# Convolution weights fetched into another buffer ahead of time, and attention run by pairs of key-value heads, in a decoder layer on eight cores

## The chip, the cores and the metric

The kernel runs on all 8 cores of one Trainium2 chip. Every core runs the same program on its own rows: 2048 prompt rows and 64 rows of new tokens, with all weights read by each core. The metric is the time on the device, in microseconds (us), of the slowest core. TensorE (PE) does the matmuls, ScalarE (ACT), VectorE (DVE) and GpSimd (POOL) the elementwise work. PE, ACT, DVE and POOL each take their instructions in program order; transfers are issued from the queues of SyncE (SP) and POOL.

## The reference

One layer. The input projection gives queries, keys, values, a gated linear unit `u` and two gates. Two branches use them: banded attention with a sink, and a causal depthwise convolution of width 31 with layer norm.

```python
def _sink_attention(q, k, v, mask, sink):
    s = jnp.einsum('nqkgd,nskd->nkgqs', q, k,
                   preferred_element_type=jnp.float32) * ATTN_SCALE
    s = jnp.where(mask, s, NEG)
    sk = sink.astype(jnp.float32).reshape(1, N_KV_HEADS, GROUP, 1, 1)
    m = jnp.maximum(jnp.max(s, axis=-1, keepdims=True), sk)
    e = jnp.exp(s - m)
    den = jnp.sum(e, axis=-1, keepdims=True) + jnp.exp(sk - m)   # sink column absorbs mass
    p = (e / den).astype(v.dtype)
    o = jnp.einsum('nkgqs,nskd->nqkgd', p, v)
    return o.reshape(o.shape[0], o.shape[1], ATT_W)
...
def _conv_tail(ubuf, conv_w, conv_b, cln_g, cln_b, w_conv_o):
    c = lax.conv_general_dilated(ubuf, conv_w[:, None, :], (1,), 'VALID',
                                 dimension_numbers=('NWC', 'WIO', 'NWC'),
                                 feature_group_count=D_CONV) + conv_b
    c = jax.nn.silu(_layernorm(c, cln_g, cln_b))
    return c @ w_conv_o
```

There are 16 query heads of 64 channels on 4 key-value heads, a window of 128, 1024 convolution channels and 2048 model channels. Then `mix = (gate0 * (attention @ w_attn_o) + gate1 * conv) @ w_out`, a residual, and a squared-ReLU MLP of 8192 channels.

## The kernel before

**Groups.** The rows of a core are worked in three groups: group 0 has 5 blocks of 128 rows and the 128 rows ahead of them, group 1 has 6 blocks, group 2 has 5 blocks and the 64 new-token rows (`G.SA`). A group goes through the whole layer before the next begins. All weights come as slabs of 2048 x 512 (`load_slab`, `prefetch`), through three buffers, from the POOL queue.

**Dense steps and side work.** A stage of dense work is a generator that stops after each output tile of 128 channels by half the group's columns: 16 matmuls into one PSUM bank, here called a dense step. `run(main, side, per)` (line 278) lets a second generator take `per` of its steps for each dense step. While attention runs, the main stages are `q_stage(G, 1)`, `ub_stage(G, 0)`, `ua_stage(G, 1)` and `ub_stage(G, 1)`, 8 dense steps each, in banks 0 to 3; banks 4 and 5 take scores, 6 transposes, 7 value products. A dense step of `q_stage` is read out by DVE, one of `ua_stage` by ACT, one of `ub_stage` by ACT (tanh into `ring`) and then by DVE, which waits for `ring`.

**Attention** (`att_stage`). A unit is one block `i` of 128 queries and one key-value head (`kv = 2a + hh`), with its 4 query heads. Head `hh` of a pair `a` lives on channels 0 to 63 or 64 to 127 of the partitions. `S`: 8 score matmuls (4 query heads by two key blocks, 64 rows of the array, 128 columns) into banks 4 and 5; ACT copies one bank to `Sp`, DVE writes the masked other one over it (`copy_predicated`), DVE takes the minimum, and ACT computes 4 exponentials with their sums. `N`: DVE reciprocal, POOL multiply. `Tr`: 4 transposes into bank 6, and DVE spreads them by the mask into `PT`. `V`: 2 value matmuls of 512 columns into one half of the output columns of bank 7; after the second head of a pair ACT or DVE reads the bank out. The loop at the end of `att_stage` runs, in step `k`, `S(k)`, `N(k-1)`, `Tr(k-3)`, `V(k-4)`. In group 2 there are 8 further units (`SUnit`) for the cached keys of the new tokens.

**Convolution** (`conv_stage`). `ub_stage` writes `u` to a scratch in HBM, 4 chunks of 128 channels at a time, once for each half (`us0`, `us1`). `load_x(ch)` reads a chunk back four times, shifted by one row each, into `X`; 4 such buffers are in use. A chunk is then 64 matmuls that use 32 of the 128 array columns each, in turns on the four quarters. The weights of a chunk are 32 x 32 blocks in HBM (`wdb`): chunks 0 and 1 are loaded into `wd0` and `wd1` before attention, chunks 2 to 5 into `wdm`, which lies in `AT`, and chunks 6 and 7 into `wd0` and `wd1` once chunks 0 and 1 are done. `AT` is the buffer that holds attention's `P` and `PT`, so the transfer of `wdm` is issued on SP after the last value product. The eight chunks run beside `gate_stage(G, 0, 0)`, one behind each of its dense steps.

## Time and profile before

| what | us |
|---|---|
| median of 3 runs | 3547.96 |
| lowest and highest | 3545.12, 3552.78 |
| the profiled execution | 3547.48 |
| its span on the slowest core (core 7) | 3545.8 |
| spans of the other cores | 3528.3 to 3543.3 |
| PE busy | 3406.3 (96%) |
| LDWEIGHTS busy | 2202.0 (62%) |
| DVE, ACT, POOL busy | 1052.7, 825.6, 478.2 |

PE is busy for 96% of the span, and most of the rest lies in three places, once in each group: the stretch in which attention runs beside the projections, and the stretch of the convolution behind it. A busy PE is not PE at its peak: the ends of matmuls are modelled, so the distance between the starts of two entries tells more than their durations. The granted clock column (PEclk) is a share of 2.4 GHz, 0.5 being 1.2 GHz.

### The profile page before, as it was taken

The page shows a single profiled execution, that of the slowest core. Times are in us where ns is not written, and L with a number is a line of the kernel's source. Part 1 is how long each engine was busy: PE and PEld are TensorE (multiplying, and loading weights), DVE is VectorE, ACT ScalarE, POOL GpSimd, SP SyncE. Part 2 cuts the span into 40 slices and gives each one's busy share as a digit, 9 for nine tenths or more (in the row PEclk, how much of TensorE's full clock was granted, in tenths as well). Part 3 has the DMA queues.
Part 4 walks back from the last instruction along what each step waited for, and adds up shares of the span by engine and source line. Part 5 has one row for each costly group of instructions (what it writes and reads, how often), then busy time and mean ns, then how long its engine had stood idle before and what let it go on. Part 6 is the DMA issues. An engine that isn't in the chain of part 4 may idle for free.

```text
span 3545.8 us, 62090 instructions; the slowest of 8 cores (3528.3 to 3545.8 us)
## 1 busy us (share of the span) xinstructions
PE 3406.3 (96%) x24208; PEld 2202.0 (62%) x24208; DVE 1052.7 (30%) x1963; ACT 825.6 (23%) x1877; POOL 478.2 (13%) x604
## 2 busy tenths in 40 slices
PE   7979999999999989999999999998889999999997
PEld 5546777777776545666666666664556666666664
DVE  2423222222234434132222222345341222222223
ACT  2443132111101444113210111113431132110103
POOL 0112020011012113003001110121130030000003
PEclk9989999999999999999999999999989999999998
DMA  8775786677778375567666666687776575565553
GB/s 173 121 145 104 138 164 125 127 144 149 141 160 188 79 144 104 111 111 146 115 114 129 131 123 112 135 163 126 139 143 130 113 157 120 121 128 105 110 118 91
DMA packets 83262, 460.61 MB, mean 130 GB/s; under 512 B 7552, under 2 KB 39936, under 8 KB 61568
## 3 DMA queue, kind: packets, MB, share of 16 engines
q0 software_dynamic: 27520, 351.48, 55.8%
q1 hardware_dynamic: 55456, 105.17, 10.7%
q8 instruction: 197, 3.23, 0.4%
q14 instruction: 89, 0.73, 0.1%
HBM read 784.43 MB, written 31.49 MB: 230 GB/s over the span
## 4 chain that ended last, share of the span: by engine, by line
PE 87%; DMA 4%; DVE 3%; ACT 3%; issue 2%; POOL 1%; SPq 0%; ACTq 0%; DVEq 0%; POOLq 0%
PE ps L130 87%; DMA AT<-wdb 2%; ACT AT L130 1%; DVE R L130 1%; DMA yT<-R 1%; DVE TMP L130 1%; DMA MIX<-xm 1%; POOL R L130 1%; ACT TMP L130 1%; ACT R L130 0%; DVE sm L130 0%; SPq L130 0%; DVE AT L130 0%; ACT ring L130 0%; ACT GT L130 0%
## 5 line engine op out<-in xcount | busy, mean ns | idle before, releaser
L130 PE MATMUL ps<-N,w 128*128 128x384 bf16 (+3 forms) x11712 | 1798.3, 315 | 0.0
L130 PEld LDWEIGHTS ps<-N,w 128*128 128x128 bf16 x11712 | 1144.4, 98 | 644.4 <-issue 39.1
L130 PE MATMUL ps<-MIX,w 128*128 128x320 bf16 (+2 forms) x4608 | 688.8, 313 | 0.0
L130 PEld LDWEIGHTS ps<-MIX,w 128*128 128x128 bf16 x4608 | 450.9, 98 | 236.5
L130 PE MATMUL ps<-GT,w 128*128 128x320 bf16 (+2 forms) x3072 | 459.4, 313 | 0.0
L130 DVE SCALAR_TENSOR_TENSOR ring<-ps,TMP 128x320 f32<-128x320 f32 (+2 forms) x384 | 200.7, 524 | 678.6 <-PE ps L130 675.4
L130 DVE TENSOR_TENSOR R<-ps,R 128x320 f32<-128x320 f32 (+2 forms) x384 | 201.4, 524 | 672.0 <-PE ps L130 672.0
L130 PEld LDWEIGHTS ps<-GT,w 128*128 128x128 bf16 x3072 | 300.6, 98 | 157.9 <-issue 0.2
L130 POOL TENSOR_TENSOR TMP<-TMP 128x320 f32<-128x320 f32 (+2 forms) x222 | 209.3, 946 | 434.7 <-ACT TMP L130 434.7
L130 PE MATMUL ps<-R,w 128*128 128x320 bf16 (+2 forms) x1536 | 232.0, 312 | 3.2 <-ACT R L130 3.2
L130 DVE SCALAR_TENSOR_TENSOR GT<-GT,ps 128x320 f32<-128x320 f32 (+2 forms) x192 | 99.5, 520 | 398.6 <-PE ps L130 387.4
L130 ACT ACTIVATE GT<-ps,hbg 128x320 f32<-128x320 f32 (+2 forms) x192 | 105.8, 552 | 435.2 <-PE ps L130 435.2
L130 ACT ACTIVATE GT<-ring 128x320 bf16<-128x320 f32 (+2 forms) x192 | 95.3, 496 | 479.5 <-DVE ring L130 479.5
L130 ACT ACTIVATE TMP<-R 128x320 f32<-128x320 f32 (+2 forms) x240 | 114.9, 488 | 395.1 <-DVE R L130 391.6
L130 ACT ACTIVATE MIX<-ring 128x320 bf16<-128x320 f32 (+2 forms) x192 | 94.7, 496 | 463.5 <-DVE ring L130 463.5
L130 PEld LDWEIGHTS ps<-R,w 128*128 128x128 bf16 x1536 | 150.0, 98 | 83.2 <-issue 4.9
L130 ACT ACTIVATE AT<-TMP,sm 128x129 bf16<-128x129 f32 (+1 forms) x264 | 107.9, 409 | 147.4 <-DVE sm L130 129.6
L130 POOL DMA_DIRECT2D w<-w_dn x48 | 25.9, 539 | 710.4 <-PE ps L130 710.4
L130 POOL DMA_DIRECT2D w<-w_up x48 | 26.3, 547 | 620.9 <-PE ps L130 620.9
L130 POOL TENSOR_TENSOR AT<-AT,sm 128x512 bf16<-128x512 bf16 x64 | 66.4, 1038 | 274.4 <-DVE sm L130 257.8
L130 DVE SCALAR_TENSOR_TENSOR R<-ps,R 128x320 f32<-128x320 f32 (+2 forms) x96 | 50.4, 525 | 176.8 <-PE ps L130 176.8
L130 ACT ACTIVATE N<-R,vec 128x320 bf16<-128x320 f32 (+2 forms) x96 | 56.4, 588 | 195.9 <-DVE R L130 195.9
(104 smaller groups left out, 1409.0 us busy)
## 6 DMA issues: line engine op xcount, KB each, us to landing
w<-w_up POOLq DMA_DIRECT2D x48, 2048.0 KB, 16.9
w<-w_dn POOLq DMA_DIRECT2D x48, 2048.0 KB, 16.3
w<-w_in POOLq DMA_DIRECT2D x45, 2048.0 KB, 15.8
w<-w_ac POOLq DMA_DIRECT2D x12, 2048.0 KB, 17.1
w<-w_out POOLq DMA_DIRECT2D x12, 2048.0 KB, 16.2
AT<-xm SPq DMA_DIRECT2D x32, 384.0 KB, 11.6
AT<-xm SPq DMA_DIRECT2D x32, 352.0 KB, 9.3
MIX<-uscr SPq DMA_DIRECT2D x52, 167.0 KB, 6.3
```

The source lines that it names most:

```text
L130: ins = getattr(engobj, fn[0])(*fn[1], **fn[2])
```

## The change

**Convolution weights.** The chunks 2 to 7 (instead of 2 to 5) go to `wdm`, which now lies in the second part of the gate buffer `GT` and is loaded on SP together with `wd0` and `wd1`, before attention begins. The reloads of `wd0` and `wd1` are gone. To make room, the tail of `u` that is an output goes through `RS`, and the tails of keys and values through `TMP`. The second half of `u` is written to the scratch two chunks at a time, the first two after half of the stage, and `load_x` waits for the write of its own chunk alone.

**Attention by twos.** A `Pair` is both key-value heads of `a` on one block. Its scores come as two steps: `A` does the later key block, 8 matmuls in turns on the row halves, head 0 into bank 4 and head 1 into bank 5, and ACT copies both; `B` does the earlier key block into the same banks, then DVE and ACT follow as before, for both heads. `Tr` does 8 transposes into the two halves of bank 6, and `V` 4 value matmuls in turns on the column halves of bank 7. There are 6 buffers for `P` instead of 4. The loop runs in step `k` first `V(k-3)`, `A(k)`, `N(k-1)`, and after a yield `Tr(k-2)`, `B(k)`. A step of the side work is thus half of a pair, `na` is 4·nb+5 (+8 in group 2) instead of 4·nb+4 (+8), and the `SUnit`s run by twos as well.

```diff
-            ut = gtf[:, 3200:3200 + 768].rearrange("p (k c) -> p k c", c=96)
+            ut = RS[:, 0:768].rearrange("p (k c) -> p k c", c=96)
...
-            hs = slice(hf * 4, hf * 4 + 4)
-            dmas("sp", [(uscr[G.g, hs, :, 0:G.UW].rearrange("k p c -> p k c"), G.uT[:, hs, :])],
-                 reads=[f"uT{c}" for c in range(hf * 4, hf * 4 + 4)], writes=[f"us{hf}"], sem=f"d_us{hf}")
-            if G.SA:
-                dmas("sp", [(sscr[hs].rearrange("k p c -> p k c"), G.ub[:, hs, :, :].rearrange("p k r b -> p k (r b)"))],
-                     reads=["ubs"] + [f"ub{c}" for c in range(hf * 4, hf * 4 + 4)], writes=[f"ss{hf}"], sem=f"d_ss{hf}")
+                if m == 3 or m == 1 and hf:
+                    h0, hs = (ch - 1, slice(ch - 1, ch + 1)) if hf else (0, slice(0, 4))
+                    dmas("sp", [(uscr[G.g, hs, :, 0:G.UW].rearrange("k p c -> p k c"), G.uT[:, hs, :])],
+                         reads=[f"uT{c}" for c in range(h0, ch + 1)], writes=[f"us{c}" for c in range(h0, ch + 1)], sem=f"d_us{ch}")
+                    if G.SA:
+                        dmas("sp", [(sscr[hs].rearrange("k p c -> p k c"), G.ub[:, hs, :, :].rearrange("p k r b -> p k (r b)"))],
+                             reads=["ubs"] + [f"ub{c}" for c in range(h0, ch + 1)], writes=[f"ss{c}" for c in range(h0, ch + 1)],
+                             sem=f"d_ss{ch}")
...
+            place("GATES", [("wdm", 12800, 25088)])
+            wm = gtb[:, 6400:12544].rearrange("p (k a b) -> p k a b", k=6, a=32)
+            dmas("sp", [(wm, wdb[2:8].rearrange("k p a b -> p k a b"))], reads=["wdb"], writes=["wdm"], sem="d_wdm")
             yield
...
-                dmas("sp", pairs, reads=[f"us{ch // 4}"] + ([f"ss{ch // 4}"] if G.SA else []), writes=[f"X{i}"], sem=f"d_X{i}")
+                dmas("sp", pairs, reads=[f"us{ch}"] + ([f"ss{ch}"] if G.SA else []), writes=[f"X{i}"], sem=f"d_X{i}")
...
             yield
-            place("AT", [("wdm", 0, 8192)])
-            wm = AT[:, 0:4096].rearrange("p (k a b) -> p k a b", k=4, a=32)
-            dmas("sp", [(wm, wdb[2:6].rearrange("k p a b -> p k a b"))], reads=["wdb"], writes=["wdm"], sem="d_wdm")
...
-                wk, wv = (f"wd{ch % 2}", wd[ch % 2][:, :, :]) if ch < 2 or ch > 5 else ("wdm", wm[:, ch - 2, :, :])
+                wk, wv = (f"wd{ch}", wd[ch][:, :, :]) if ch < 2 else ("wdm", wm[:, ch - 2, :, :])
...
                 if xl < 8:
                     load_x(xl)
                     xl += 1
-                if ch < 2:
-                    load_wd(ch + 6, wk)
...
-                def S(self):
...
-                    sp = Sp[s2][:, :, 0:128]
-                    do("pool", "tensor_copy", ["cst"], [f"sp{s2}"], out=Sp[s2][:, :, 128], in_=nsk[:, self.kv * 4:self.kv * 4 + 4])
-                    bb = [bank("S"), bank("S")]
-                    for blk in (1, 0):
-                        for g in range(4):
-                            do("pe", "matmul", ["kT", f"q{a}_{i}"], [f"ps{bb[blk]}"], inc=(g == 3), out=ps[bb[blk]][:, g * 128:g * 128 + 128],
+            class Pair:
+                def __init__(self, k, i, a):
+                    self.k, self.i, self.a = k, i, a
+                    self.s3 = [(k % 3) * 2 + j for j in range(2)]
+
+                def scores(self, blk):
+                    i, a = self.i, self.a
+                    for g in range(4):
+                        for j in range(2):
+                            hs = slice(j * 64, j * 64 + 64)
+                            b = rings["S"][j]
+                            do("pe", "matmul", ["kT", f"q{a}_{i}"], [f"ps{b}"], inc=(g == 3), out=ps[b][:, g * 128:g * 128 + 128],
                                lhsT=G.qT[hs, a * 4 + g, i * 128:i * 128 + 128],
                                rhs=G.kT[hs, a, (i + blk) * 128:(i + blk) * 128 + 128], start=True, stop=True)
-                    do("act", "activation", [f"ps{bb[1]}"], [f"sp{s2}"], out=sp, in_=ps[bb[1]][:, :].rearrange("p (g c) -> p g c", g=4),
-                       func=AF.Copy)
-                    do("dve", "copy_predicated", [f"ps{bb[0]}", "msk", f"sp{s2}"], [f"sp{s2}"], out=sp, mask=mpv,
-                       data=ps[bb[0]][:, :].rearrange("p (g c) -> p g c", g=4))
-                    if G.g == 0 and i == 0:
-                        do("dve", "tensor_tensor", ["msk", f"sp{s2}"], [f"sp{s2}"], out=sp, in0=sp, in1=mad, op=ALU.add)
-                    do("dve", "tensor_reduce", [f"sp{s2}"], [f"nm{s3}"], out=sm[:, 0, s3, :], in_=Sp[s2], axis=AX.X, op=ALU.min)
-                    for g in range(4):
-                        do("act", "activation", [f"sp{s2}", f"nm{s3}"], [f"P{s3}_{g}", f"dn{s3}"], out=Pb[s3][:, g, 0:129],
-                           in_=Sp[s2][:, g, :], func=AF.Exp, scale=-1.0, bias=sm[:, 0, s3, g:g + 1],
-                           accum_out=sm[:, 1, s3, g:g + 1])
+
+                def A(self):
+                    self.scores(1)
+                    for j in range(2):
+                        b = rings["S"][j]
+                        do("act", "activation", [f"ps{b}"], [f"sp{j}"], out=Sp[j][:, :, 0:128],
+                           in_=ps[b][:, :].rearrange("p (g c) -> p g c", g=4), func=AF.Copy)
+                    for j in range(2):
+                        kv = 2 * self.a + j
+                        do("pool", "tensor_copy", ["cst"], [f"sk{j}"], out=Sp[j][:, :, 128], in_=nsk[:, kv * 4:kv * 4 + 4])
+
+                def B(self):
+                    self.scores(0)
+                    for j in range(2):
+                        b, s3, sp = rings["S"][j], self.s3[j], Sp[j][:, :, 0:128]
+                        do("dve", "copy_predicated", [f"ps{b}", "msk", f"sp{j}"], [f"sp{j}"], out=sp, mask=mpv,
+                           data=ps[b][:, :].rearrange("p (g c) -> p g c", g=4))
+                        if G.g == 0 and self.i == 0:
+                            do("dve", "tensor_tensor", ["msk", f"sp{j}"], [f"sp{j}"], out=sp, in0=sp, in1=mad, op=ALU.add)
+                        do("dve", "tensor_reduce", [f"sp{j}", f"sk{j}"], [f"nm{s3}"], out=sm[:, 0, s3, :], in_=Sp[j], axis=AX.X, op=ALU.min)
+                        for g in range(4):
+                            do("act", "activation", [f"sp{j}", f"sk{j}", f"nm{s3}"], [f"P{s3}_{g}", f"dn{s3}"], out=Pb[s3][:, g, 0:129],
+                               in_=Sp[j][:, g, :], func=AF.Exp, scale=-1.0, bias=sm[:, 0, s3, g:g + 1],
+                               accum_out=sm[:, 1, s3, g:g + 1])
...
                 def Tr(self):
-                    s2, s3 = self.s2, self.s3
-                    b = bank("T")
-                    for g in range(4):
-                        do("pe", "transpose", [f"P{s3}_{g}", "msk"], [f"ps{b}"], inc=(g == 3), out=psb[b][:, g * 128:g * 128 + 128],
...
+                    b = rings["T"][0]
+                    for j, s3 in enumerate(self.s3):
+                        for g in range(4):
+                            do("pe", "transpose", [f"P{s3}_{g}", "msk"], [f"ps{b}"], inc=(g == 3),
+                               out=psb[b][:, j * 512 + g * 128:j * 512 + g * 128 + 128], in_=Pb[s3][:, g, 0:128], identity=idb[:, :])
+                    for j in range(2):
+                        do("dve", "tensor_tensor", [f"ps{b}", "msk"], [f"PT{j}"],
+                           out=PT[j].rearrange("p (b g q) -> p b g q", b=2, g=4),
+                           in0=psb[b][:, j * 512:j * 512 + 512].rearrange("p (g q) -> p g q", g=4).unsqueeze(1).broadcast_to([128, 2, 4, 128]),
+                           in1=mkq, op=ALU.mult)
...
                     for blk in (1, 0):
-                        do("pe", "matmul", [f"v{i + blk}", f"PT{s2}"], [f"ps{b}"], inc=(blk == 0), out=ps[b][self.hs, :],
-                           lhsT=G.vt[:, i + blk, self.kv * 64:self.kv * 64 + 64], rhs=PT[s2][:, (1 - blk) * 512:(2 - blk) * 512],
-                           start=(blk == 1), stop=(blk == 0))
-                    if self.hh == 1:
-                        evac([f"ps{b}"], [f"q{a}_{i}"], G.qT[:, a * 4:a * 4 + 4, i * 128:i * 128 + 128],
-                             ps[b][:, :].rearrange("p (g q) -> p g q", g=4))
+                        for j in range(2):
+                            kv = 2 * a + j
+                            do("pe", "matmul", [f"v{i + blk}", f"PT{j}"], [f"ps{b}"], inc=(blk == 0 and j == 1), out=ps[b][j * 64:j * 64 + 64, :],
+                               lhsT=G.vt[:, i + blk, kv * 64:kv * 64 + 64], rhs=PT[j][:, (1 - blk) * 512:(2 - blk) * 512],
+                               start=(blk == 1), stop=(blk == 0))
...
             n = len(units)
-            for k in range(n + 4):
-                if G.SA and k in (2, 9):
-                    make_qc(k > 2)
+            for k in range(n + 3):
+                if 0 <= k - 3 < n:
+                    units[k - 3].V()
                 if k < n:
-                    units[k].S()
+                    units[k].A()
                 if 0 <= k - 1 < n:
                     units[k - 1].N()
-                if 0 <= k - 3 < n:
-                    units[k - 3].Tr()
-                if 0 <= k - 4 < n:
-                    units[k - 4].V()
+                yield
+                if G.SA and k in (1, 4):
+                    make_qc(k > 2)
+                if 0 <= k - 2 < n:
+                    units[k - 2].Tr()
+                if k < n:
+                    units[k].B()
                 yield
...
-            na = 4 * G.nb + 4 + (8 if G.SA else 0)
+            na = 4 * G.nb + 5 + (8 if G.SA else 0)
...
```

What stands in a row on TensorE in group 0, beside the first dense steps of `ub_stage(G, 0)`: `ps<-N,w` is a dense step (`x32` are two), `ps<-R` scores, `ps<-idb,AT` transposes, `ps<-AT,R` value products. Before:

```order
L130 MATMUL ps<-N,w 128x336 x32
L130 MATMUL ps<-R 128x128 x8
L130 MATMUL ps<-idb,AT 128x128 x4
L130 MATMUL ps<-AT,R 64x512 x2
L130 MATMUL ps<-N,w 128x336 x16
```

and after:

```order
L130 MATMUL ps<-N,w 128x336 x32
L130 MATMUL ps<-AT,R 64x512 x4
L130 MATMUL ps<-R 128x128 x8
L130 MATMUL ps<-N,w 128x336 x16
L130 MATMUL ps<-idb,AT 128x128 x8
L130 MATMUL ps<-R 128x128 x8
L130 MATMUL ps<-N,w 128x336 x16
```

Where each gap between dense steps held the scores, transposes and value products of one unit each, the gaps now hold in turn value products with scores of a pair, and transposes with scores of a pair; the 8 score matmuls alternate between two banks.

VectorE in the same stage, from one unit to the next (the `ring` rows are readouts of dense steps, `ps4` and `ps5` the scores, `ps6` the transposes). Before:

```order
L130 SCALAR_TENSOR_TENSOR R2<-ring1,GT 128x336
L130 COPY_PREDICATED TMP<-msk,ps4 128x4x128
L130 TENSOR_REDUCE sm<-TMP 128x4
L130 RECIPROCAL sm<-sm 128x4
L130 TENSOR_TENSOR AT<-ps6,msk 128x1024
L130 SCALAR_TENSOR_TENSOR R2<-ring0,GT 128x336
```

and after:

```order
L130 TENSOR_TENSOR AT<-ps6,msk 128x1024 x2
L130 COPY_PREDICATED TMP<-msk,ps4 128x4x128
L130 TENSOR_REDUCE sm<-TMP 128x4
L130 COPY_PREDICATED TMP<-msk,ps5 128x4x128
L130 TENSOR_REDUCE sm<-TMP 128x4
L130 SCALAR_TENSOR_TENSOR R2<-ring0,GT 128x336
L130 RECIPROCAL sm<-sm 128x4 x2
L130 SCALAR_TENSOR_TENSOR R2<-ring1,GT 128x336
```

The reciprocals stood behind the minimum of the next unit and now stand ahead of it; the readout of the transposes stood behind the scores and now stands ahead of them, and a dense readout that waits for ScalarE lies between the minimum of one pair and the scores of the next.

The SP queue in group 0, from the first convolution weights on (`wdb` weights, `uscr` the scratch of `u`). Before:

```order
L130 DMA wd<-wdb 128x1024 x2
L130 DMA uscr<-R 128x4x672
L130 DMA MIX<-uscr 32x4x668 x16
L130 DMA uscr<-R 128x4x672
L130 DMA AT<-wdb 128x4x1024
L130 DMA MIX<-uscr 32x4x668 x4
L130 DMA wd<-wdb 128x1024
```

and after:

```order
L130 DMA wd<-wdb 128x1024 x2
L130 DMA GT<-wdb 128x6x1024
L130 DMA uscr<-R 128x4x672
L130 DMA MIX<-uscr 32x4x668 x16
L130 DMA uscr<-R 128x2x672 x2
L130 DMA MIX<-uscr 32x4x668 x16
```

The block of weights moved from behind the last write of `u` to ahead of the first, the write of the second half became two, and nothing but the loads of chunks stands behind them.


## Rows read from the trace of the kernel before

**Rows 1.** Busy time by stretch: the three attention stretches, columns as its head says.
```profile
core 7: us, PE busy (x) PEld busy (x) DVE busy (x) ACT busy (x) POOL busy (x), PEclk, DMA share, GB/s
106.68:226.54 119.86, 108.49 (x761) 64.93 (x761) 57.14 (x110) 62.03 (x210) 24.96 (x41) 0.91 0.65 113
1170.28:1302.43 132.15, 119.31 (x817) 65.45 (x817) 64.28 (x123) 73.28 (x247) 29.66 (x49) 0.97 0.49 92
2403.30:2552.18 148.88, 122.52 (x961) 70.55 (x961) 77.23 (x195) 71.28 (x243) 25.96 (x42) 0.94 0.66 120
```

**Rows 2.** The same view, the three convolution stretches.
```profile
226.54:277.77 51.23, 38.26 (x641) 25.74 (x640) 6.47 (x14) 18.52 (x39) 11.38 (x13) 0.87 0.70 140
1302.43:1357.40 54.97, 45.36 (x642) 25.77 (x641) 7.32 (x14) 20.83 (x39) 13.46 (x13) 0.91 0.71 143
2552.18:2618.23 66.05, 47.13 (x898) 30.79 (x897) 7.14 (x16) 20.94 (x46) 12.41 (x13) 0.82 0.87 174
```

**Rows 3.** Waits of PE over the whole span: us in total, times, longest.
```profile
PE ps L130 <- DMA AT<-wdb: 34.9, 3, 13.0
```

**Rows 4.** Timeline of PE in convolution: start, us, engine, form, count [idle before].
```profile
228.82 2.36 PE L130 MATMUL ps<-MIX,wd 128*32 128x320 bf16 x64
231.11 2.35 PE L130 MATMUL ps<-N,w 128*128 128x320 bf16 x16
...
250.99 4.02 PE L130 MATMUL ps<-MIX,AT 128*32 128x320 bf16 x64 [12.97 <-DMA AT<-wdb]
...
2590.17 0.24 PE L130 MATMUL ps<-MIX,AT 128*32 128x64 bf16 x4 [4.67 <-issue]
```

**Rows 5.** Timeline of the SP queue at the start of that stretch.
```profile
227.48 0.38 SPq L130 DMA_DIRECT2D uscr<-R  x1
228.02 1.01 SPq L130 DMA_DIRECT2D AT<-wdb  x1
246.47 1.74 SPq L130 DMA_DIRECT2D MIX<-uscr  x4
```

**Rows 6.** Transfers issued in 105:290 us: count, KB each, median us to landing.
```profile
MIX<-uscr SPq DMA_DIRECT2D x32, 167.0 KB, 8.7
...
uscr<-R SPq DMA_DIRECT2D x2, 672.0 KB, 11.3
...
AT<-wdb SPq DMA_DIRECT2D x1, 1024.0 KB, 22.7
```

**Rows 7.** Timeline of PE, one unit of attention between dense steps.
```profile
163.00 0.62 PE L130 MATMUL ps<-R 64*128 64x128 bf16 x8
163.55 0.40 PE L130 MATMUL ps<-idb,AT 128*128 128x128 bf16 x4
163.88 0.62 PE L130 MATMUL ps<-AT,R 128*64 128x512 bf16 x2
164.43 4.73 PE L130 MATMUL ps<-N,w 128*128 128x336 bf16 x32
```

**Rows 8.** Timeline of PE, scores of a new-token unit and what follows.
```profile
2463.39 0.30 PE L130 MATMUL ps<-MIX 64*32 64x256 bf16 x4
...
2463.63 0.40 PE L130 MATMUL ps<-idb,AT 128*128 128x128 bf16 x4
```

**Rows 9.** Timeline of DVE and ACT from one unit's exponentials to the next unit's.
```profile
191.11 0.66 DVE L130 TENSOR_TENSOR AT<-ps,msk 128x1024 bf16<-128x1024 bf16 x1
191.20 0.41 ACT L130 ACTIVATE AT<-TMP,sm 128x129 bf16<-128x129 f32 x1 [1.73 <-DVE sm L130]
...
193.37 0.43 ACT L130 ACTIVATE GT<-ps 128x336 f32<-128x336 f32 x1
...
193.70 0.58 ACT L130 ACTIVATE TMP<-ps 128x512 f32<-128x512 f32 x1
194.38 0.73 DVE L130 COPY_PREDICATED TMP<-msk,ps 128x512 f32<-128x512 int16 x1 [2.01 <-ACT TMP L130]
...
196.01 0.41 ACT L130 ACTIVATE AT<-TMP,sm 128x129 bf16<-128x129 f32 x1 [1.72 <-DVE sm L130]
```

More of the change, by code:

```diff
@@ L232, in build @@
         tf = TMP[:, :]
-        Pb = [AT[:, i * 520:(i + 1) * 520].rearrange("p (g c) -> p g c", g=4) for i in range(4)]
-        PT = [AT[:, 2080 + i * 1024:2080 + (i + 1) * 1024] for i in range(2)]
+        Pb = [AT[:, i * 520:(i + 1) * 520].rearrange("p (g c) -> p g c", g=4) for i in range(6)]
+        PT = [AT[:, 3120 + i * 1024:3120 + (i + 1) * 1024] for i in range(2)]
         atf = AT[:, :].bitcast(F32)
@@ new lines, in N @@
+                def N(self):
+                    for s3 in self.s3:
+                        do("dve", "reciprocal", [f"dn{s3}"], [f"rd{s3}"], out=sm[:, 2, s3, :], in_=sm[:, 1, s3, :])
+                        do("pool", "tensor_tensor", [f"rd{s3}"] + [f"P{s3}_{g}" for g in range(4)], [f"P{s3}_{g}" for g in range(4)],
+                           out=Pb[s3][:, :, 0:128], in0=Pb[s3][:, :, 0:128], in1=sm[:, 2, s3, :].unsqueeze(2).broadcast_to([128, 4, 128]),
+                           op=ALU.mult)
@@ L835, in V @@
                         hs = slice(hh * 64, hh * 64 + 64)
-                        out = ps[b][hs, a * 32:a * 32 + 32]
+                        out = ps[b][hs, o0 + a * 32:o0 + a * 32 + 32]
                         vc = slice(kv * 64, kv * 64 + 64)
```

102 lines of the change are left out of this document (54 added, 48 removed).

## The prediction

> **What bounds the kernel now.** I read the page for the share of PE (96% of the span), then the waits of PE, then the busy time by stretch around them. Two kinds of stretch stand out, once in each group. In the three stretches of attention [rows 1] PE's window is 119.86 + 132.15 + 148.88 = 400.9 us. In the three of the convolution [rows 2] it is 51.23 + 54.97 + 66.05 = 172.3 us. Everything else in the program is dense work that the change doesn't touch. So the sum is made of these 573 us, and the rest of the profiled execution (3547.48 us, of which the span is 3545.8) is carried over. It stands 0.5 us below the median of the runs, so what I subtract from the one I subtract from the other.
>
> **Convolution, what is removed.** PE waits 34.9 us in three waits for `AT<-wdb` [rows 3]. The queue shows why: that transfer is issued at 228.02, behind the last write of `u` and 0.8 us ahead of the first convolution matmul, and takes 22.7 us to land [rows 5, 6]. Moved ahead of attention it has over 100 us. What would the stretch be without it? A chunk of 64 matmuls takes 231.11 - 228.82 = 2.29 us at 320 columns [rows 4], which is also about what a dense step of 16 matmuls takes, since the four column quarters work at once. Eight chunks and eight dense steps are then 16 x 2.29 = 36.6 us in group 0; scaled by the columns (384 in group 1; 352 in group 2, whose chunk has 704 in all) 43.9 and 40.3 us. That leaves 14.6 + 11.1 + 25.8 = 51.5 us of the 172.3 as excess. It is the 34.9 us of waits, the slow clock behind them (the first chunk after the wait takes 4.02 us for 2.36 [rows 4]; the granted clock is 0.87, 0.91 and 0.82 in the three stretches [rows 2]), and, in group 2, waits that the profile lays on nothing, the longest 4.67 us [rows 4].
>
> **Convolution, what is late next.** The loads of chunks 4 to 7. Before, the load of chunk 4 was issued at 246.47, when the write of the whole second half of `u` had landed, 19 us after its issue at 227.48 [rows 5]. With no stall chunk 4 is due four chunk-and-step periods of 4.58 us after 228.82, at 247.1, so the old order would have waited here for the chunk's 8.7 us to landing [rows 6]: without the second edit, the first would return some 8 us per group. With it, chunks 4 and 5 are written four dense steps earlier and their loads wait for a free buffer only, from 231.1 on: 16 us for a transfer of 8.7. Chunk 6 needs the last write, now half as large; if it still takes 19 us it lands at 246.5, and 8.7 us later, at 255.2, the chunk is there, due at 256.3. That is tight, and in group 2 the DMA share is 0.87 [rows 2]. Removing the 22.7 us transfer from the same moments helps. I take 47 of the 51.5 us, and 30 to 52 as the bounds: the low end gives back some 7 us per group for a late chunk. The early transfer, now 1.5 times as large, itself is free: what stands behind it on SP is the first write of `u`, due only at the end of `ub_stage(G, 0)`, and PE's one wait for a transfer in these stretches is the one removed [rows 3]. The moved tails of `u`, keys and values are the same instructions on other buffers that are idle then.
>
> **Attention, PE's work.** One unit is 0.55 us of scores, 0.33 of transposes and 0.55 of value products, from start to start [rows 7]: 1.43 us. A dense step is 4.73 / 2 = 2.37 us at 336 columns, so 2.26, 2.71 and 2.48 at 320, 384 and 352. From the first scores on, the stretches hold 30, 30 and 31 dense steps, 20, 24 and 20 units and, in group 2, 8 new-token units of about 0.9 us (an estimate: 0.24 us for their scores [rows 8], the rest in proportion). PE's work is thus 99 + 116 + 112 = 327 us of 400.9; 74 us are waits and slow clock. What do turns on the row and column halves save? For columns, the convolution shows four quarters at once [rows 4]. For rows the nearest row is the new-token scores: 4 matmuls of 256 columns on two row halves and four column quarters take 0.24 us with 4 small ones from start to start [rows 8], where one alone, at a dense step's 0.148 us for 336 columns, would take 0.11 us and four 0.45. So I take both halves as working at once: a pair has 0.55 us of scores for 1.10, 0.55 of values for 1.10, 0.66 of transposes as before; 1.77 us for 2.86. Over 32 pairs this is 35 us less work (17 if the row halves do not overlap, 0 if neither).
>
> **Attention, the chain.** Less PE work is less time only where PE is the limit. From one unit's first exponential to the next unit's it is 196.01 - 191.20 = 4.81 us [rows 9]: 2.17 for four exponentials, 0.33 for a dense readout on ACT, 0.68 for the copy of scores, 1.63 for masking and minimum on DVE until ACT starts. Two units are 9.6 us, while PE's work for two with their dense steps is 9.2, 9.1 and 7.8 us in the three groups. Test: 24, 28 and 32 steps of 4.81 us are 115, 135 and 154 us, against 120, 132 and 149 measured. So the chain, not PE, sets the pace, barely in groups 0 and 1. After the change the chain per pair is, by the same rows:
> in `q_stage` and `ua_stage`: 8 exponentials 4.5, dense readout 0.33 (not in `q_stage`), two copies 0.68 + 0.55, the pair's second scores on PE, which wait for the copies, 0.35, masking and minimum of the first head 1.63, and half a value readout 0.3: 8.0 and 8.3 us;
> in `ub_stage`: 4.5, 0.33, 1.23, a second tanh 0.33, the DVE readout that waits for it 0.6, two readouts of transposes 2 x 0.57 [rows 9] that now stand ahead of the scores, 1.63 and 0.3: 10.0 us.
> PE's work per pair is 7.8, 7.8 and 6.6 us, below all of them. By the program's order the pairs fall 3, 3, 3 and 1 on the four stages in group 0, 3, 4, 3 and 2 in group 1, 4, 1, 3 and 2 in group 2, which has 4 new-token pairs at PE's pace (2 x 2.48 + 1.8 = 6.8). Behind the last scores the rest is PE's: 17, 17 and 18 us. Sum: group 0 3 x 8.0 + 3 x 10.0 + 3 x 8.3 + 10.0 + 17 = 106; group 1 24 + 40 + 25 + 20 + 17 = 126; group 2 32 + 10 + 25 + 20 + 27 + 18 = 132. Together 364 for 400.9: 37 us less. Bounds: 5 us less, where the chain is no better than before, and 75 less, where PE's 292 us and some 34 of waits are all that is left.
>
> **The sum.** 3547.96 - 47 - 37 = 3464 us.
>
> The Trainium skill (TensorEngine Tiling (Array Packing), section Tiling Modes) says that changing the tiling mode drains TensorE. Here the rows show a start 2.29 us after the last for the chunk between dense steps, 64 matmuls at full pace [rows 4], so no drain that counts. By the page the change would gain a little more: the switches of mode fall from 8 to 5 per pair, 3 x 0.07 us (a score matmul's tail, 0.62 - 0.55 [rows 7]) x 32 = 7 us, 3457.
>
> **The rivals.**
> 1. The chain takes all of the attention gain. Speaking for it: DVE now reads transposes and waits for a `ring` ahead of the scores, and a block of eight exponentials holds ACT for 4.5 us, in which nothing else is read out. If a q or ua pair also takes 9.6 us, attention is within 10 us of before: 3547.96 - 47 - 5 = 3496. The Trainium skill (TensorEngine Tiling (Array Packing), section Performance Considerations, PSUM Bottleneck) has the rule that tiling speeds up TensorE but not the evacuation of PSUM; by that rule the trace agrees as far as the 9.6 us chain over 9.2 us of PE work goes.
> 2. A late chunk takes the place of the late weights: 30 us instead of 47 in the convolution, 3481; with 5 us more lost per group, 3496.
> 3. The row halves do not overlap, so the change doesn't do what it says: 17 us more PE work, of which the chain hides most, 0.28 us per pair on it: 32 x 0.28 = 9, 3473.
> 4. The blocks mesh better than I have them, since PE runs ahead within a double dense step: attention at 326, 3426.
> 5. Slower: the granted clock. PE would be idle for 2.2 of 10 us in `ub_stage`, and a wait of 12.97 us left the next chunk at 4.02 us for 2.36 [rows 4]. Attention is at 0.91, 0.97 and 0.94 now [rows 1]. With 292 us of work it gives back all 84 us and more only if the mean clock there falls below 292 / 448 = 0.65; at 0.60 the stretches are 487 us and the time is 3547.96 - 47 + 86 = 3587.
>
> **How the numbers follow.** Forecast (with 3, which lies in its range, 3446 to 3483) 0.56; rival 1 0.20; rival 2 0.08; rival 4 0.11; rival 5 0.03; nothing gained at all 0.02. The range 3424 to 3504 holds all but rival 5, the last and the outer part of rivals 1 and 4. A measurement tells about 0.2% (7 us) from no change. Faster by more than that 0.95, within it 0.02, slower 0.03.
>
> **What would show each step right or wrong.** No wait of PE for a transfer of `wdb`, and convolution stretches of 37 to 40, 44 to 47 and 40 to 47 us; if rival 2 holds, waits for `MIX<-uscr` instead. Scores of a pair 0.28 us from start to start for 8, value products 0.55 for 4. Exponential to exponential 8.0 to 8.3 us per pair beside `q_stage` and `ua_stage`, 10 beside `ub_stage`, and PE's waits there ended by ACT's copies and DVE's `AT`. Attention stretches of about 106, 126 and 132 us at a clock over 0.9. The forecast is wrong if one of the three stays at its old length, or if the time saved in them is lost again in the dense work behind, where PE has no waits now.

## The result, and the profile after

The changed kernel takes 3501.39 us (median of 4 runs, 3498.03 to 3667.09), the kernel before 3549.04 (4 runs, 3545.12 to 3552.78) on the same chip. The ratio is 0.9864, with a 95% interval of 0.9846 to 0.9881: 48 us faster, where 84 were forecast. In the run of 3667.09 us the cores of one die had a mean granted clock of 0.94 instead of 0.99; ratios, and the times given below, leave such executions out.

The profiled execution took 3500.47 us, with a span of 3498.9 on core 2. Its busy time by stretch, the three of attention and then the three of the convolution, answers to [rows 1, 2]:

```profile
core 2: us, PE busy (x) PEld busy (x) DVE busy (x) ACT busy (x) POOL busy (x), PEclk, DMA share, GB/s
108.16:219.50 111.34, 94.24 (x761) 59.10 (x761) 60.07 (x111) 61.45 (x211) 27.26 (x42) 0.97 0.76 142
1151.35:1282.74 131.39, 109.39 (x818) 61.39 (x817) 69.86 (x124) 72.63 (x249) 31.33 (x50) 0.96 0.49 96
2372.84:2518.17 145.33, 120.01 (x962) 69.24 (x961) 85.37 (x197) 69.79 (x243) 27.34 (x43) 0.89 0.70 137
219.50:257.71 38.21, 38.21 (x641) 25.47 (x641) 6.05 (x13) 17.94 (x37) 10.79 (x12) 0.96 0.71 135
1282.74:1326.10 43.36, 43.36 (x641) 24.83 (x641) 6.85 (x13) 19.93 (x37) 12.89 (x12) 1.00 0.68 133
2518.17:2571.42 53.25, 43.80 (x898) 29.33 (x897) 6.46 (x13) 20.74 (x45) 11.81 (x12) 0.95 0.87 170
```

The convolution stretches lose 13.0, 11.6 and 12.8 us, 37.4 in all, and those of attention 8.5, 0.8 and 3.6, 12.9 in all. What lies around them grew by 3.4 us. Together that is the 46.9 us between the spans. This sets the slowest core of one kernel (7) against the slowest of the other (2); the means over the eight cores are close to it, 35.1 us for the convolution and 11.0 for attention.

In the attention rows PE is busy for 323.6 us in place of 350.3, so 26.7 us of its work went, which is what working on both halves of the array at once was to bring. But the stretches are only 12.9 shorter, so PE stands idle for 13.8 us more. VectorE's busy time rose, with the same instructions, from 198.7 to 215.3 us (the column in [rows 1] and here), and GpSimd's from 80.6 to 85.9. That is the clue to what follows. The waits of PE over the whole span (us, times, longest), where [rows 3] had the transfer of `wdb`:

```profile
PE ps L130 <- ACT TMP L130: 34.4, 38, 2.9
PE ps L130 <- ACT R L130: 25.0, 8, 11.7
PE ps L130 <- DVE AT L130: 19.9, 14, 4.8
PE ps L130 <- issue: 9.6, 7, 3.7
PE ps L130 <- DVE TMP L130: 9.1, 13, 1.3
PE ps L130 <- POOL TMP L130: 4.9, 1, 4.9
```

These six are all that the trace has. `ACT TMP` are the copies of the first scores, which must have left banks 4 and 5 before the second scores go there. `DVE TMP` are the predicated copies of the pair before, which hold the same banks against the next first scores. One pair beside `ub_stage` of group 1 on PE, from its second scores to the next pair's first (answers to [rows 7]):

```profile
1199.84 0.61 PE L130 MATMUL ps<-idb,AT 128*128 128x128 bf16 x8
1202.24 0.21 PE L130 MATMUL ps<-R 64*128 64x128 bf16 x1 [1.79 <-ACT TMP L130]
1202.73 0.58 PE L130 MATMUL ps<-R 64*128 64x128 bf16 x7 [0.27 <-ACT TMP L130]
1203.24 4.14 PE L130 MATMUL ps<-N,w 128*128 128x384 bf16 x16
1207.31 0.62 PE L130 MATMUL ps<-AT,R 128*64 128x512 bf16 x4
1207.87 0.46 PE L130 MATMUL ps<-R 64*128 64x128 bf16 x8
1208.26 2.77 PE L130 MATMUL ps<-N,w 128*128 128x384 bf16 x16
```

Two things cost here: the wait, and the slow dense step behind it (4.14 us for 2.77; the granted clock is 0.65 from 1203.24 to 1207.31 and 1.00 in the dense step at 1208.26). The same moment on the other engines (answers to [rows 9]):

```profile
1200.65 0.47 ACT L130 ACTIVATE ring<-ps 128x384 f32<-128x384 f32 x1
1201.02 0.59 ACT L130 ACTIVATE R<-ps 128x512 bf16<-128x512 f32 x1
1201.22 0.56 DVE L130 SCALAR_TENSOR_TENSOR R<-ring,GT 128x384 bf16<-128x384 f32 x1 [3.59 <-ACT ring L130]
1201.50 1.08 ACT L130 ACTIVATE TMP<-ps 128x512 f32<-128x512 f32 x2
1201.70 0.23 DVE L130 RECIPROCAL sm<-sm 128x4 f32<-128x4 f32 x2
1202.02 2.04 POOL L130 TENSOR_TENSOR AT<-AT,sm 128x512 bf16<-128x512 bf16 x2 [0.95 <-DVE sm L130]
1202.45 0.51 ACT L130 ACTIVATE ring<-ps 128x384 f32<-128x384 f32 x1
1203.13 1.33 DVE L130 SCALAR_TENSOR_TENSOR R<-ring,GT 128x384 bf16<-128x384 f32 x1 [1.20 <-ACT ring L130]
1204.39 1.27 DVE L130 TENSOR_TENSOR AT<-ps,msk 128x1024 bf16<-128x1024 bf16 x2
1205.59 0.71 DVE L130 COPY_PREDICATED TMP<-msk,ps 128x512 f32<-128x512 int16 x1
...
1207.31 0.41 ACT L130 ACTIVATE AT<-TMP,sm 128x129 bf16<-128x129 f32 x1 [4.35 <-DVE sm L130]
```

Three queues stand behind one another. ScalarE's copies (1201.50) come behind eight exponentials, a tanh and a value readout. VectorE waits at the head of its queue for that tanh, 3.59 us. And the product of the second tanh takes 1.33 us for the 0.56 of the first: it runs beside the second of GpSimd's two multiplications by one over the sum (the row of 2.04 us holds both). Behind it stand the readout of transposes, both predicated copies and, 4.35 us idle, ScalarE.

The Trainium skill (SBUF — State Buffer, section Who interferes with whom) says that a VectorE instruction with two SBUF inputs contends with a GpSimd instruction that reads SBUF, and that the port pair which they share is an exclusive lock. The trace agrees: the product reads `ring` and `GT`, and ends about 0.4 us after the second multiplication, at 1204.46.

### The profile page after: what moved, and what is told of

Same layout as the page of the kernel before. It is cut to its first block, busy times and chain, and to the rows that moved or that the text cites. A ratio compares the mean times of both kernels' runs of the same rounds, so it can differ in the third digit from the quotient of the medians.

```text
span 3498.9 us, 62212 instructions; the slowest of 8 cores (3487.0 to 3498.9 us)
## 1 busy us (share of the span) xinstructions
PE 3377.9 (97%) x24208; PEld 2189.3 (63%) x24208; DVE 1066.9 (30%) x1963; ACT 821.5 (23%) x1877; POOL 482.3 (14%) x604
## 4 chain that ended last, share of the span: by engine, by line
PE 90%; DVE 3%; ACT 3%; issue 2%; DMA 1%; POOL 0%; SPq 0%; ACTq 0%; DVEq 0%; POOLq 0%
PE ps L130 90%; ACT AT L130 2%; DVE R L130 1%; DMA MIX<-xm 1%; DVE TMP L130 1%; DVE AT L130 1%; ACT TMP L130 0%; DVE sm L130 0%; POOL R L130 0%; ACT R L130 0%; ACT ring L130 0%; SPq L130 0%; ACTq L127 0%; DVEq L127 0%; ACT L130 0%
## 5 line engine op out<-in xcount | busy, mean ns | idle before, releaser
L130 DVE SCALAR_TENSOR_TENSOR ring<-ps,TMP 128x320 f32<-128x320 f32 (+2 forms) x384 | 200.7, 524 | 678.9 <-PE ps L130 677.2
L130 POOL DMA_DIRECT2D w<-w_in x45 | 25.1, 557 | 450.6 <-PE ps L130 397.4
## 6 DMA issues: line engine op xcount, KB each, us to landing
w<-w_in POOLq DMA_DIRECT2D x45, 2048.0 KB, 15.7
```

The costliest lines, as they stand in the source:

```text
L130: ins = getattr(engobj, fn[0])(*fn[1], **fn[2])
```

## The experiments

The experiments ran on other chips than the pair above. The kernel before, run beside them, took 3546 to 3549 us there (medians; beside `e13` single runs went from 3543.5 to 3563.7), so a difference of some 3 us between two of them says nothing. `e5` and `e13` leave work out and have no ratio on record.

**The two halves apart.** `e1` is the kernel before with the new `ub_stage`, `kv_stage` and `conv_stage`; `e2` is the changed kernel with the old three.

> The kernel before with the convolution half of the change alone: weights loaded early into GATES, u written to DRAM in three pieces, tail in RS; attention as before. Theory T (the two halves are independent, the traces give -37.3 us for the three convolution stretches): 3549 - 37 = 3512, range 3507 to 3518, with no wait AT <- wdb in the trace. Rival R (part of the convolution's gain came from attention ending in a better place, and the early weight load steals from attention): 3520 to 3530.

Measured: 3513.8 us, ratio 0.9913 (0.9897 to 0.9928): 31 us, in T's range, and as T has it PE has no wait for `wdb` in its trace.

> The changed kernel with the convolution half undone: attention by pairs, weights of the convolution fetched as before. Theory T (additive; traces give -12.9 us for the three attention stretches): 3549 - 13 = 3536, range 3531 to 3541; the wait of TensorE for wdb is back at about 35 us in all. Rival R (attention by twos is worth the forecast 37 us, and the early weights took 24 of it back by load on DMA and memory): 3512 to 3520.

Measured: 3524.9 us, ratio 0.9940 (0.9926 to 0.9954): 21 us, more than T's 13 and less than R's 37. The attention stretches are as in the changed kernel (383.6 to 386.9 us by core, for 382.4 to 389.9), so the early weights take nothing from them. But its convolution stretches are shorter than before, 152.7 to 163.4 us by core for 162.3 to 173.1. On core 3:

```profile
PE ps L130 <- DMA AT<-wdb: 26.0, 3, 10.6
```

PE waits 26.0 us for the weights and not 34.9 [rows 3] (by core 17.5 to 26.6 us for 28.7 to 38.3). The transfer is issued 2.07 us ahead of the first convolution matmul (218.11 and 220.18), before 0.80 us ahead [rows 4, 5]. Before, it stood behind the write of `u` at 227.48, which itself came after the last value products; in `e2` PE waits 1.75 us for VectorE ahead of them (they start at 216.90), the write goes out in that time, at 216.12, and the transfer follows the value products at once. So the halves overlap: 31 + 21 us apart, 48 together. The convolution half is 27 to 31 of them, the attention half 17 to 21 by this subtraction, some of which shows in the convolution.

**Are the turns on the row halves the gain?**

```diff
-                    for g in range(4):
-                        for j in range(2):
+                    for j in range(2):
+                        for g in range(4):
```

> The changed kernel, but the eight score matmuls of a half step are issued head by head (four on rows 0-63, then four on rows 64-127) and not in turns. Each set of eight should take 0.55 us again in place of 0.33, 64 sets, so 14 us more of busy TensorE. Theory T (the chain over ScalarE and VectorE sets the pace, TensorE has waits to give): 3501 + 3 to 8 us. Rival R (TensorE's own time is the limit and the turns are the whole gain of the attention half): 3501 + 13 to 16 us.

Measured: 3494.2 us, ratio 0.9852 (0.9834 to 0.9871): not slower at all, so both theories fell, and their common premise with them. Eight first scores in this order, on core 0:

```profile
1213.49 0.41 PE L130 MATMUL ps<-R 64*128 64x128 bf16 x8
1213.83 2.77 PE L130 MATMUL ps<-N,w 128*128 128x384 bf16 x16
```

They take 0.34 us to the next start, as in turns (0.39 and, in other pairs, 0.33), while eight on one row half took 0.55 [rows 7]. What is worth 0.2 us is that both halves are used, not that they alternate. The intervals of this kernel and the changed one overlap, so no gain is claimed.

**What stands in the chain?** `e4` queues the second scores, with masking, minimum and exponentials, ahead of the transposes:

```diff
-                    units[k - 2].Tr()
-                if k < n:
                     units[k].B()
+                if 0 <= k - 2 < n:
+                    units[k - 2].Tr()
```

> The changed kernel, but in the second half step the second scores with their masking, minimum and exponentials are queued ahead of the transposes and masking multiplies of the pair two before. Theory T (the chain score copy, second scores, predicated copy, minimum, exponentials, next score copy sets the pace, and the two VectorE multiplies of about 0.5 us each stand in it): up to 1.1 us of each of 32 pairs, 3501 - 5 to - 20 us. Rival R (the path goes through transposes and value products, or TensorE): 3501 + 0 to + 10 us.

Measured: 3505.0 us, ratio 0.9883 (0.9864 to 0.9902), inside R. PE's waits on core 3:

```profile
PE ps L130 <- DVE AT L130: 47.9, 41, 4.6
...
PE ps L130 <- ACT TMP L130: 12.3, 12, 2.9
```

The wait that T aimed at fell from 34.4 to 12.3 us, and the one for the readouts of transposes rose from 19.9 to 47.9. The chain gave the time to another chain on the same engine. An order that only swaps two things on VectorE is no way out.

**GpSimd beside VectorE.** Two kernels take the product out of the multiplication's way. `e5` leaves the multiplication of prompt pairs out (the 2.04 us of its expectation are two multiplications; one takes 1.02):

```diff
-                        do("pool", "tensor_tensor", [f"rd{s3}"] + [f"P{s3}_{g}" for g in range(4)], [f"P{s3}_{g}" for g in range(4)],
-                           out=Pb[s3][:, :, 0:128], in0=Pb[s3][:, :, 0:128], in1=sm[:, 2, s3, :].unsqueeze(2).broadcast_to([128, 4, 128]),
-                           op=ALU.mult)
```

> The changed kernel without GpSimd's multiplication of the prompt pairs' probabilities by one over their sum (so the output lacks that scaling); the reciprocals stay. 64 operations of about 2.04 us on GpSimd go. Theory T (they stretch VectorE's readouts of the sigmoid product, 0.56 us alone and 1.2 to 1.4 us beside a multiply, but these are few): the long readouts are back at 0.6 us, the tail of each attention stretch 1 to 2 us shorter, 3501 - 3 to - 8 us. Rival R (the two engines hindering each other is what took the missing gain): 3501 - 12 to - 24 us.

`e12`, run when `e8` below was known, keeps it, half a step later:

```diff
-                if 0 <= k - 1 < n:
-                    units[k - 1].N()
                 yield
...
                     units[k].B()
+                if 0 <= k - 1 < n:
+                    units[k - 1].N()
                 yield
```

> The changed kernel with one thing of e8 alone: the reciprocals and GpSimd's multiplication of a pair are queued half a step later (end of the second half step of the next pair); exponentials, buffers and turns stay. In the changed kernel VectorE waits 12 us for exponentials at the reciprocals in group 2's attention stretch alone, and the sigmoid products behind them run beside the multiplication, at 0.77 us for 0.46. Theory T (this is a cost of its own, the one that leaving the multiplication out took away): VectorE busy in the three stretches 215 to about 200 us, 3501 - 5 to - 18 us. Rival R (all of e8's 31 us is the order on ScalarE): 3501 - 3 to + 5 us.

Measured: 3480.3 us for `e5`, and 3479.5, ratio 0.9807 (0.9791 to 0.9824), for `e12`: 20 and 21 us below the changed kernel. For `e5` that is rival R, for `e12` just past T. Groups of VectorE instructions over the whole span (busy us, mean ns, idle before); the changed kernel:

```profile
L130 DVE SCALAR_TENSOR_TENSOR R<-ring,GT 128x384 bf16<-128x384 f32 x16 | 13.1, 821 | 29.5 <-ACT ring L130 29.2
L130 DVE RECIPROCAL sm<-sm 128x4 f32<-128x4 f32 x64 | 9.5, 168 | 42.9 <-ACT AT L130 42.9
```

`e5`, core 7:

```profile
L130 DVE RECIPROCAL sm<-sm 128x4 f32<-128x4 f32 x64 | 9.5, 168 | 41.2 <-ACT AT L130 41.2
L130 DVE SCALAR_TENSOR_TENSOR R<-ring,GT 128x384 bf16<-128x384 f32 x16 | 8.9, 556 | 32.5 <-ACT ring L130 32.2
```

`e12`, core 7:

```profile
L130 DVE SCALAR_TENSOR_TENSOR R<-ring,GT 128x384 bf16<-128x384 f32 x16 | 8.9, 556 | 34.1 <-ACT ring L130 33.9
L130 DVE RECIPROCAL sm<-sm 128x4 f32<-128x4 f32 x64 | 7.4, 158 | 0.0
```

Both bring the product from 821 ns back to 556, its length before the change too, and VectorE's busy time in the three stretches from 215.2 to 215.8 us by core down to 200.7 to 201.5 in `e5` and 198.2 to 198.7 in `e12`. VectorE's 42 us of idleness at the reciprocals stay in `e5` and go from there in `e12` (some 26 us turn up ahead of the two kinds of masking instructions instead), with the same time, so that idleness was not what cost. `e5` also drops the multiplication's own latency; but its results are read by the transposes alone, and in the changed kernel PE has no wait for them (it would read `POOL AT`). What is left is the hindrance: some 12 us of stretched products (all shapes), in a place where the masking, the exponentials and the next scores stand behind them, with the clock behind the waits. In `e12` PE still waits 29.3 us for the copies.

**The exponentials out of the way.** `e8` adds to `e12`'s edit four score buffers for two, and queues a pair's exponentials half a step later, behind the next pair's copies. `e9` is `e8` with the scores head by head.

```diff
                 if k < n:
                     units[k].A()
                 if 0 <= k - 1 < n:
-                    units[k - 1].N()
+                    units[k - 1].E()
                 yield
```

> The changed kernel with four score buffers for two, and the eight exponentials of a pair queued half a step later, behind the score copies of the next pair; the scaling by one over the sum follows half a step later too. Theory T (the second scores wait for copies that stand behind eight exponentials on ScalarE, 34 us in all, and for the bank that VectorE reads, 9 us): both waits fall to under 10 us in all, attention stretches 386 to 355 to 370 us, 3501 - 12 to - 30 us. Rival R (ScalarE has as much work as before, so the wait moves to the transposes or to dense readouts): 3501 - 6 to + 6 us, with waits of TensorE for ACT AT or ACT R instead.

> e8 with the scores head by head in place of turns. Theory T (in the changed kernel turns cost because the first head's second scores wait for the second head's copy too, 0.28 us or more per pair; with the copies early that wait is gone): same as e8 within 3 us. Rival R (turns cost by themselves, whatever is waited for): e8 - 5 us or more.

Measured: 3469.7 us, ratio 0.9784 (0.9770 to 0.9798), and 3468.6, 0.9780 (0.9767 to 0.9794). The time is T's, 1 us past the end of its range: 31 us, of which `e12` has 21 and the exponentials 10; and the turns are worth nothing here either. Attention is at 354.4 to 359.0 us by core. But of the waits only one part came true. On core 2 of `e8`:

```profile
PE ps L130 <- DVE AT L130: 22.6, 22, 2.8
PE ps L130 <- DVE TMP L130: 15.7, 18, 1.7
```

The wait for the copies is gone, and the one for the bank that VectorE reads grew from 9.1 to 15.7 us. Two further kernels go for these two. `e10` is `e9` with both minima behind both predicated copies; `e11` is `e10` with four exponentials in each half step:

```diff
                         do("dve", "copy_predicated", [f"ps{b}", "msk", f"sp{x}"], [f"sp{x}"], out=sp, mask=mpv,
                            data=ps[b][:, :].rearrange("p (g c) -> p g c", g=4))
+                    for j in range(2):
+                        s3, x = self.s3[j], self.q + j
...
                         do("dve", "tensor_reduce", [f"sp{x}", f"sk{x}"], [f"nm{s3}"], out=sm[:, 0, s3, :], in_=Sp[x], axis=AX.X, op=ALU.min)
```

```diff
+                    units[k - 1].E(0)
                 yield
+                if 0 <= k - 1 < n:
+                    units[k - 1].E(1)
```

> e9 with the two minima of a pair queued behind both predicated copies on VectorE, so that the second score bank is free 0.7 us earlier. Theory T (the first scores of the next pair wait for that bank, VectorE TMP 11 us in all, up to 1.3 us a time): this wait under 5 us, 3468 - 3 to - 8 us. Rival R (the exponentials of the first head, now 0.7 us later, or the value products bind): 3468 - 2 to + 3 us.

> e10 with the eight exponentials split: four in the first half step, four in the second, so that a tanh of a dense step stands behind four and not eight. Theory T (VectorE waits for that tanh at the head of its queue, 5 us a time, and the value products wait for VectorE, 18 us in all): waits for DVE AT under 10 us in all, 3468 - 8 to - 18 us. Rival R (ScalarE has the same work in a pair, so the order inside it is worth nothing more): within 3 us of e10.

Measured: 3457.8 us, ratio 0.9743 (0.9729 to 0.9758), 11 us less than `e9`; and 3428.9 us, 0.9664 (0.9648 to 0.9680), another 29 less. Both exceed their T. In `e10` the wait for the bank fell to 1.4 us. In `e11`, on core 1, the attention stretches of groups 0 and 1, and two of PE's waits over the whole span (the second was 19.7 to 21.3 us on the cores of `e10` looked at):

```profile
106.70:198.62 91.92, 89.06 (x761) 57.26 (x761) 55.16 (x111) 62.45 (x211) 25.62 (x40) 1.00 0.94 171
1127.65:1233.86 106.21, 102.62 (x818) 58.81 (x817) 60.97 (x124) 73.61 (x249) 30.08 (x48) 1.00 0.61 120
```

```profile
PE ps L130 <- issue: 9.8, 6, 3.7
PE ps L130 <- DVE AT L130: 8.6, 8, 2.0
```

ScalarE has as much to do as ever (62.45 and 73.61 us); PE is busy for 97% of both, at full clock. A pair with its two dense steps takes 1196.35 - 1189.26 = 7.09 us beside `ua_stage`, all of it matmuls. Only here does the lighter work of the twos pay in full. This kernel is 72 us faster than the changed one and 120 faster than the one before.

**The waits for nothing in group 2's convolution.** In the changed kernel, runs of matmuls break off in the middle, nearly all in this stretch (answers to the last of [rows 4]; core 2):

```profile
2528.01 2.56 PE L130 MATMUL ps<-MIX,wd 128*32 128x320 bf16 x90
2534.30 0.29 PE L130 MATMUL ps<-MIX,wd 128*32 128x64 bf16 x6 [3.74 <-issue]
2534.52 3.88 PE L130 MATMUL ps<-N,w 128*128 128x352 bf16 x16
```

`e7` moves the store of `u_o` behind the chunks; `e13` leaves out 20 of the loads. Its condition `ch < nb` keeps those of chunks 0 to 2: group 2 has three chunk buffers, not the four of the other groups.

```diff
+            if G.SA:
+                dmas("sp", [(u_o[:, :, :], RS[:, 0:768].rearrange("p (k c) -> p k c", c=96))], reads=["RS0", "RS1"], sem="d_o2")
             yield
```

```diff
-                    if G.SA:
+                    if G.SA and ch < nb:
                         src = sscr[ch].rearrange("(g c) w -> c g w", c=32)[:, :, 16 * tap:16 * tap + 512]
```

> The changed kernel, but the store of the tail of u (the output u_o, 128 x 8 x 96) is issued behind the convolution of group 2 and not at its start. Theory T (TensorE's waits for nothing in group 2's convolution, 4 to 9 us on the cores, come from a DMA system that is 0.87 busy, and this store of small pieces is a share of it): convolution stretch of group 2 from 52 to 47 to 50 us, 3501 - 2 to - 5 us. Rival R (the store is too small to matter): within 2 us of 3501.

> The changed kernel, leaving out the loads of the new-token windows from sscr for convolution chunks 3 to 7 of group 2 (20 transfers of 128 KB; their part of the convolution then works on the values of earlier chunks), so that the stretch moves 2.6 MB less at the same matmuls. In that stretch TensorE waits 6.2 to 9.7 us on the cores of the changed kernel for nothing that the profile shows. Theory T (those waits come from the DMA system, 0.87 busy there): they fall to 3 us or less, the stretch from 50.5 to 53.9 us to 45 to 48, 3501 - 3 to - 7 us. Rival R (they come with this stretch's matmuls or with loads in general, not with their amount): 6 to 10 us of such waits as before, the stretch over 50 us, within 2 us of 3500.

Measured: `e7` 3496.3 us, ratio 0.9862 (0.9848 to 0.9876), its stretch at 50.1 to 53.1 us by core. The time is 5 us under 3501, at the edge of T; but the ratio is that of the changed kernel (0.9864), and the stretch did not come down to T's 47 to 50. Nothing can be told apart, as R has it. `e13` 3490.0 us, 10 less. On core 3:

```profile
2509.20:2552.00 42.80, 40.63 (x898) 28.15 (x897) 6.46 (x13) 20.94 (x45) 11.84 (x12) 1.00 0.66 149
```

```profile
2519.78 0.23 PE L130 MATMUL ps<-MIX,wd 128*32 128x64 bf16 x6 [0.68 <-issue]
```

By core the stretch takes 42.8 to 49.9 us and these waits 2.2 to 6.4, for 50.5 to 53.9 and 6.2 to 9.7. With the same matmuls and less to move the waits halve (3.7 us for 7.6, means of the cores; T had 3 or less) and the stretch is 6.6 us shorter (mean), about as T has it. That the time fell by 10 us rather than 7 lies within what the chips differ by.

Where the waits went says more than their sum. The 34 stops of over 0.4 us in the changed kernel, over all cores, lie at six places only, the same six in the order of PE's matmuls on every core, 125 or 126 matmuls apart. In `e13` those at the first two places are as long as before (26.1 us in all for 19.8; the six matmuls shown above wait 0.68 us for 0.91 on core 3, but 4.01 for 3.74 on core 2), at the third they fell from 9.4 to 3.4 us, and at the last three, where the loads left out would run, they are gone (30.9 us before). So they come from the load on the DMA system at that moment; the share of a whole stretch doesn't tell them (core 0 has 0.59, and waits 6.4 us).

What is late are instructions. The trace also has the transfers of the kind `instruction`. On core 2 of the changed kernel, in the stretch (2518 to 2572) and just ahead of the longest wait (2532 to 2533; queue, packets, MB, share):

```profile
q8 instruction: 8, 0.13, 1.1%
q8 instruction: 1, 0.02, 6.0%
```

They are packets of 16 KB. The one of the second row ends at 2532.99, and PE goes on at 2534.30; each of the 34 restarts comes 1.3 to 1.8 us after the end of such a packet, and each of the 18 in `e13` 1.1 to 1.6 us. The Trainium skill (Runtime: NRT & Kernel Launch, section Instruction fetch mechanics) says that each engine's sequencer fetches its instructions in blocks of 16 KiB over a DMA queue of its own. The trace agrees in the size of the packets and in the even distance of the stops.

## Why the prediction was right and wrong

**The total** lies in the range (3424 to 3504) and near its upper end. The forecast case (3446 to 3483) did not come; rival 1, the chain that takes the attention gain, did by its number, 3496. That number is in part luck: rival 1 had 47 us from the convolution and 5 from attention, and wanted pairs of 9.6 us beside `q_stage` and `ua_stage`. Measured were 37.4 and 12.9 us, 3.4 us were lost elsewhere, and of those pairs (table below) only the ones beside `ua_stage` in group 0 (10.4 us each) are that long; the others take 7.8 to 8.7.

**Convolution, removal and next wait: right.** The term was 47 us (30 to 52) and measured 37.4. No wait for `wdb`; 38.2 and 43.4 us in groups 0 and 1, for 37 to 40 and 44 to 47. Rival 2 did not come: no PE wait for `MIX<-uscr`, and on two cores one of 2.5 and 1.2 us for `sscr`. No run takes the early weights and the write of `u` in pieces apart, so what the second of them is worth (8 us per group by the prediction) stays open. **Group 2: mis-sized.** The stretch takes 53.25 us for 40 to 47; of the 25.8 us that I called excess there, 12.8 went. I had counted the waits on nothing as part of the stall; they are instructions that come late under the load of the transfers, which the change leaves as it is, 9.6 us in all on this core (`e13`).

**Attention, PE's work: right in kind, somewhat less in size** (26.7 us at the clock as granted; 35 at full clock were forecast. In `e11`, near full clock, PE is busy for 297.6 to 300.0 us in the three stretches, for the 292 that I had as its work.) Four value products take 0.56 us, as forecast, eight scores 0.33 for 0.28. It isn't the turns that do it: use of both halves does, in either order (`e3`).

**Attention, the chain: the step that failed.** The term was 37 us and measured 12.9. The sum can be laid beside the trace, from the start of one pair's step (the value products ahead of its first scores) to that of a later one (us, in groups 0, 1 and 2):

| pairs beside | forecast | changed, core 2 | `e12`, core 7 |
|---|---|---|---|
| `q_stage` (group 2: and one more) | 24, 24, 42 | 25.4, 23.5, 43.3 | 25.4, 24.8, 41.5 |
| `ub_stage(G, 0)` | 30, 40 | 30.1, 44.0 | 30.7, 42.3 |
| new-token pairs | 27 | 36.3 | 35.4 |
| `ua_stage` | 25, 25, 25 | 31.2, 26.2, 23.6 | 27.2, 25.0, 23.4 |
| `ub_stage(G, 1)` | 10, 20, 20 | 6.7, 19.8, 21.3 | 6.7, 19.8, 20.4 |
| the rest | 17, 17, 18 | 18.0, 17.9, 20.8 | 15.5, 15.5, 14.5 |

I added a pair's chain from durations of before, 0.6 us for the product that waits for a tanh. In the changed order it meets GpSimd's multiplications and takes 1.33. That is worth 20 us over all rows (`e12`; 16 in attention in `e5`): I checked each queue for what stands in it, not what runs beside it. The largest miss in one place is another, the new-token pairs, which I priced at PE's pace, without a chain:

```profile
2416.16:2452.43 36.27, 31.73 (x256) 18.14 (x256) 25.09 (x72) 13.92 (x49) 3.04 (x4) 0.91 0.44 74
```

They take 36.3 us on every core, no less than the 8 units before (36.8 us on core 7, from 2454.28 to 2491.09). `e12` gives back 0.9 us of it, so it isn't GpSimd; VectorE is busy for 25.1 us of the 36.3, but what holds them no run here isolates. Next, the chain with eight exponentials ahead of the copies of scores was priced as 10.0 us per pair beside `ub_stage`, and takes 11.0 in group 1 (the first scores shown at 1207.87 come 11.5 us ahead of the next pair's, 1219.38). The wait of the first scores for the bank under the predicated copy wasn't in the sum at all (9.1 us here, 15.7 in `e8`). And the clock fell to 0.89 in group 2 on this core (0.94 before), rival 5's mechanism in a small dose; the 0.65 at which it would decide was far off.

**The dense work behind** is as it was: 3.4 us more over the program, no new wait.

## What to carry to other kernels

When an edit makes the bound engine's work lighter, it pays only as far as the order on the engines that feed it allows: the pairing brought the stretches of attention from 400.9 us to 388.1, and changes of order with two more buffers (scaling later, exponentials behind the copies and in halves, minima last) brought them to 313.9 to 320.3 by core. Cost an instruction in the new order by what will run beside it, too, above all VectorE instructions with two SBUF inputs beside GpSimd. Cut long bursts on an engine that also does short readouts for others into pieces: four exponentials and four, instead of eight, were worth 29 us with not one instruction less.

## What the runs showed of the hardware

- Eight score matmuls take 0.33 us in turns on both row halves, 0.34 head by head, and 0.55 on one half. Alternation is not what makes them overlap.
- A VectorE product of two SBUF tensors of 384 columns takes 0.56 us, and 1.33 to 1.42 beside GpSimd multiplications of 1.02 to 1.18 us.
- PE stops for up to 3.74 us in the middle of a run of matmuls in a stretch with a DMA share of 0.87, at places 125 or 126 matmuls apart, and goes on 1.3 to 1.8 us after a packet of 16 KB of instructions has ended. Where `e13` leaves loads out, these stops are gone.
